# The state-space scan of a hybrid encoder step, computed feature-major: two heads in the two column halves of TensorE, the carried part in the same accumulation

## The reference, cut to what matters

```python
    w = jnp.einsum('bcign,bcjgn->bcijg', cm, bm)[..., None] * decay
    y = jnp.einsum('bcijgh,bcjghp->bcighp', w, xdt)
    ...
    y = y + jnp.einsum('bcign,bcghpn->bcighp', cm, h_in) * jnp.exp(acs)[..., None]
    ...
    y = y + d_skip.astype(jnp.float32).reshape(N_GROUPS, HEADS_PER_GROUP, 1) * xs.astype(jnp.float32)
    y = y.reshape(bsz, T, D_SSD).astype(x.dtype) * jax.nn.silu(z_b)
    y = rmsnorm(y.reshape(bsz, T, N_GROUPS, D_SSD // N_GROUPS), ...)
    o_b = y @ w_o_ssd
```

## Time and profile before

| what | value |
|---|---|
| time, median of 3 runs | 2502.21 us (2500.35 to 2502.59) |
| span of the profiled execution | 2502.9 us |
| TensorE busy, whole span | 2346.0 us (94%) |
| VectorE, ScalarE, GpSimd busy | 755.6 us (30%), 795.0 us (32%), 619.2 us (25%) |
| mean granted clock of TensorE | 0.970 |
| scan stage, first and last matmul | 1828.39 us, about 2272 us |

### The profile page before, as it was taken

The page is one execution under the profiler, slowest core; times in us unless marked ns, Lnnn a source line. Parts: engine busy times, 40 slices in busy tenths (PEclk is TensorE's granted clock), DMA queues, the critical chain, the costliest instruction groups (busy, mean ns, idle before and its releaser), DMA issues. The chain is left out here.

```text
span 2502.9 us, 35437 instructions
## 1 busy us (share of the span) xinstructions
PE 2346.0 (94%) x12807; PEld 2107.6 (84%) x12807; DVE 755.6 (30%) x1470; ACT 795.0 (32%) x1892; POOL 619.2 (25%) x547
## 2 busy tenths in 40 slices
PE   6999999999999999999999399999749999996999
PEld 5999999999999999999999278888537788774887
DVE  4211000024444000100000465555255665653221
ACT  5211111134444111221111365555245455432000
POOL 3110101110111011011010255555246655651000
PEclk9999999999999999999999599999969999998999
DMA  4311111111111212111129654444265656534432
GB/s 160 87 57 69 63 75 69 68 69 69 68 69 69 85 51 78 69 69 69 69 85 43 150 129 117 109 108 105 77 187 149 160 159 176 162 84 152 142 126 97
DMA packets 280002, 250.10 MB, mean 100 GB/s; under 512 B 74184, under 2 KB 257336, under 8 KB 272760
## 3 DMA queue, kind: packets, MB, share of 16 engines
q1 hardware_dynamic: 279944, 249.34, 35.0%
HBM read 158.35 MB, written 90.95 MB: 100 GB/s over the span
## 5 line engine op out<-in xcount | busy, mean ns | idle before, releaser
L74 PE MATMUL acc<-h_hi,w_hi 128*128 128x424 f32 (+1 forms) x2280 | 810.6, 356 | 10.1 <-DVE h_lo L547 10.1
L75 PE MATMUL acc<-h_lo,w_hi 128*128 128x424 f32 (+1 forms) x2280 | 807.5, 354 | 0.0
L76 PE MATMUL acc<-h_hi,w_lo 128*128 128x424 f32 (+1 forms) x2280 | 807.2, 354 | 0.0
L74 PEld LDWEIGHTS acc<-h_hi,w_hi 128*128 128x128 f32 x2280 | 430.3, 189 | 24.8 <-DVE h_lo L547 11.4
L75 PEld LDWEIGHTS acc<-h_lo,w_hi 128*128 128x128 f32 x2280 | 430.6, 189 | 7.3
L76 PEld LDWEIGHTS acc<-h_hi,w_lo 128*128 128x128 f32 x2280 | 430.4, 189 | 7.4
L318 POOL TENSOR_TENSOR w_lo<-w_raw,w_hi 128x1024 fp32r<-128x1024 f32 x57 | 144.7, 2539 | 1130.5 <-ACT w_hi L360 1130.5
L385 ACT ACTIVATE row<-acc 128x424 f32<-128x424 f32 (+1 forms) x215 | 112.7, 524 | 825.2 <-PE acc L76 825.1
L583 DVE SCALAR_TENSOR_TENSOR conv_acc<-conv_in,conv_wb,conv_acc 128x424 f32<-128x424 f32 (+2 forms) x216 | 126.1, 584 | 380.9 <-ACT conv_acc L430 373.1
L1113 ACT ACTIVATE a_prob<-a_score,a_neg_max 128x129 f32<-128x129 f32 x264 | 103.3, 399 | 50.3 <-DVE a_neg_max L1254 47.6
L74 PE MATMUL a_o_ps<-a_w_hi,a_at_hi 128*128 128x512 f32 (+1 forms) x272 | 117.0, 430 | 2.0 <-DVE a_branch L1287 2.0
(11 more groups left out here) (215 smaller groups left out, 3047.5 us busy)
## 6 DMA issues: line engine op xcount, KB each, us to landing
proj<-row SPq DMA_DIRECT2D x56, 1056.0 KB, 4.0
w_raw<-in_w_in_dram SPq DMA_DIRECT2D x28, 1024.0 KB, 5.1
s_feat<-proj SPq DMA_DIRECT2D x16, 1280.0 KB, 7.9
s_acs_b<-acs_dram SPq DMA_DIRECT2D x16, 1024.0 KB, 7.3
a_q_diag<-proj SPq DMA_DIRECT2D x66, 128.0 KB, 4.4
a_z<-proj SPq DMA_DIRECT2D x16, 512.0 KB, 4.8
a_gate_t<-proj SPq DMA_DIRECT2D x16, 512.0 KB, 4.6
branch_rows<-a_branch SPq DMA_DIRECT2D x16, 512.0 KB, 3.2
```

The source lines that it names most:

```text
L74: pe.matmul(out, hi, whi, start=first, stop=False)
L75: pe.matmul(out, hi, wlo, start=False, stop=False)
L76: return pe.matmul(out, lo, whi, start=False, stop=last)
```

## The change

The scan result is made with features on the partitions from the start. Each head's product has the head's 64 features as the stationary operand's columns, and even and odd heads write to partitions 0 to 63 and 64 to 127 of `y_ps`, which now has one bank for each group. The carried part goes into the same accumulation: ScalarE makes `exp(acs)` for all 16 heads on all partitions (`carried_exps`), VectorE multiplies it by C (`carried`), and each head's state times that goes into `y_ps` ahead of the chunk's part. The scaling and adding on VectorE (L1929, L1936) and the transposes (`turned`) go; `skipped` reads `y_ps`. VectorE adds the squares of four feature blocks (`square_sums`), and `squares` is one product for each group in place of four. In stage 1 one exponential and a fifth of a table go.

```diff
@@ project_inputs @@
-                    act.activation(into, acs, ACT.Exp).then_inc(exps_ready, 1)
@@ scan_states: tiles @@
-        tmp = sb("tmp", [P, BANK])
-        work = sb("work", [P, 4, D])
-        tok, yx, yg = work[:, 0, :], work[:, 1, :], work[:, 2, :]
-        y_sq = work[:, 3, :]
+        carry_c = sb("carry_c", [P, NH, P])
+        y_sum = sb("y_sum", [P, G, P])
+        work = sb("work", [P, 3, D])
+        yx, yg, y_sq = (work[:, i, :] for i in range(3))
-        y_ps = pb("y_ps", [P, BANK])
-        i_ps = pb("i_ps", [P, BANK])
+        y_ps = pb("y_ps", [P, G, BANK])
@@ SyncE: load_acs @@
                 after(sp, S["segs"], m)
-                sp.dma_start(acs_b[0:t.n, :, 0:t.n],
-                             io.acs_dram[:, bass.ds(t.col, t.n)].partition_broadcast(t.n)).then_inc(S["acs_in"], 16)
+                after(sp, S["c_exps"], m)
+                sp.dma_start(acs_b[:, :, 0:t.n],
+                             io.acs_dram[:, bass.ds(t.col, t.n)].partition_broadcast(P)).then_inc(S["acs_in"], 16)
@@ ScalarE @@
+            def carried_exps(m):
+                t = TokenTile(m)
+                act.wait_ge(S["acs_in"], 16 * m + 16)
+                after(act, S["inter_ready"], 2 * m)
+                act.activation(carry_c[:, :, 0:t.n], acs_b[:, :, 0:t.n], ACT.Exp).then_inc(S["c_exps"], 1)
...
             act.wait_ge(S["tables_in"], 16)
             decays(0, 0)
+            carried_exps(0)
...
                     decays(m + 1, 1 - slot)
                     rows_of_gb(m + 1, 1 - slot)
+                    carried_exps(m + 1)
@@ VectorE @@
-            def combine(m, slot, g):
...
+            def carried(m, slot):
+                t = TokenTile(m)
+                dve.wait_ge(S["c_exps"], m + 1)
+                dve.wait_ge(feat_in[slot], arrived(m, slot))
+                for g in range(G):
+                    v = carry_c[:, g * GH:(g + 1) * GH, 0:t.n]
+                    dve.tensor_tensor(v, v, feat[:, slot, C0 + g, 0:t.n].unsqueeze(1).to_broadcast([P, GH, t.n]),
+                                      ALU.mult).then_inc(S["c_ready"], 1)
+            def update(m, g):
                 st = state[:, stream(m), g * GF:(g + 1) * GF]
                 dve.wait_ge(S["added_ready"], 2 * m + g + 1)
                 dve.wait_ge(S["decayed"], 2 * m + g + 1)
                 dve.tensor_tensor(st, st, st_ps[:, :], ALU.add).then_inc(S["state_ready"], 1)
+            def square_sums(m):
+                t = TokenTile(m)
+                dve.wait_ge(S["ysq_ready"], 2 * m + 2)
+                after(dve, S["ss_ready"], m)
+                dve.tensor_reduce(y_sum[:, :, 0:t.n],
+                                  y_sq.rearrange("p (g k n) -> p g n k", g=G, k=GT)[:, :, 0:t.n, :],
+                                  AX.X, ALU.add).then_inc(S["ysum_ready"], 1)
             def skipped(m, slot, g):
-                dve.wait_ge(S["t_ready"], 2 * m + g + 1)
+                dve.wait_ge(S["intra_ready"], 2 * m + g + 1)
...
             masked(0, 0)
+            carried(0, 0)
             for q in range(1, 6):
                 scale_w(q)
             def step(m, slot):
-                combine(m, slot, 0)
+                if has_prev(m):
+                    square_sums(m - 1)
+                update(m, 0)
                 if has_prev(m, 2):
                     merge(m - 2, slot, 1)
-                combine(m, slot, 1)
+                update(m, 1)
                 skipped(m, slot, 0)
...
                 skipped(m, slot, 1)
                 if has_next(m):
                     times_dt(m + 1, 1 - slot, 1)
+                    carried(m + 1, 1 - slot)
                 if has_prev(m):
                     merge(m - 1, 1 - slot, 0)
@@ TensorE @@
             def core(m, slot, g):
                 after(pe, S["state_ready"], 2 * m - 2 + g + 1)
-                after(pe, S["tmp_ready"], 2 * m + g)
-                pe.matmul(i_ps[r, :], feat[:, slot, C0 + g, 0:t.n], state[:, stream(m), g * GF:(g + 1) * GF],
-                          start=True, stop=True).then_inc(S["inter_ready"], 1)
+                pe.wait_ge(S["c_ready"], 2 * m + g + 1)
+                after(pe, S["yx_ready"], 2 * m - 2 + g + 1)
+                for h in range(GH):
+                    o = slice(h % 2 * HEAD, h % 2 * HEAD + HEAD)
+                    f = g * GF + h * HEAD
+                    mm = pe.matmul(y_ps[o, g, h // 2 * P:h // 2 * P + t.n], state[:, stream(m), f:f + HEAD],
+                                   carry_c[:, g * GH + h, 0:t.n], start=(h < 2), stop=False)
+                mm.then_inc(S["inter_ready"], 1)
...
-                after(pe, S["tok_ready"], 2 * m + g)
                 for h in range(GH):
+                    o = slice(h % 2 * HEAD, h % 2 * HEAD + HEAD)
                     f = g * GF + h * HEAD
-                    mm = pe.matmul(y_ps[r, h * HEAD:(h + 1) * HEAD], mix[r, slot, g * GH + h, 0:t.n],
-                                   xdt[r, slot, f:f + HEAD], start=True, stop=True)
+                    mm = pe.matmul(y_ps[o, g, h // 2 * P:h // 2 * P + t.n], xdt[r, slot, f:f + HEAD],
+                                   mix[r, slot, g * GH + h, 0:t.n], start=False, stop=(h >= GH - 2))
...
             def gates(m, slot, h):
-                if h == 0:
-                    pe.wait_ge(g_in[slot], arrived(m, slot))
-                    after(pe, S["gate_ready"], 2 * m)
-                    pe.wait_ge(S["yx_ready"], 2 * m + 2)
-                elif t.sample:
-                    pe.wait_ge(S["gate_ready"], 2 * m + 1)
-                else:
-                    pe.wait_ge(S["yx_ready"], 2 * m + 4)
+                pe.wait_ge(g_in[slot], arrived(m, slot))
+                after(pe, S["gate_ready"], 2 * m + h)
-            def turned(m, g):
...
             def squares(m):
-                pe.wait_ge(S["ysq_ready"], 2 * m + 2)
+                pe.wait_ge(S["ysum_ready"], m + 1)
                 pe.wait_ge(S["state_ready"], 2 * min(m + 2, TILES + 1) if isinstance(m, int) else 2 * m + 4)
                 for g in range(G):
-                    for k in range(GT):
-                        f = (g * GT + k) * P
-                        mm = pe.matmul(st_ps[0:t.n, g:g + 1], y_sq[:, f:f + t.n], ones[:, 0:1],
-                                       start=(k == 0), stop=(k == GT - 1))
+                    mm = pe.matmul(st_ps[0:t.n, g:g + 1], y_sum[:, g, 0:t.n], ones[:, :], start=True, stop=True)
...
                 core(m, slot, 1)
                 if has_next(m):
                     products(m + 1, 1 - slot)
-                turned(m, 0)
                 if has_next(m):
                     x_rows(m + 1, 1 - slot, 0)
                 if has_prev(m):
                     squares(m - 1)
                 prev(run, 0, 1)
-                turned(m, 1)
```

More of the change, by code:

```diff
@@ L126, in project_inputs @@
         dt_a, t1, t2, t3 = (table(xs_flat, i) for i in range(4))
-        dt, acs, into = (table(x_more[:, :], i) for i in range(3))
+        dt, acs = (table(x_more[:, :], i) for i in range(2))
         to_end, total = (table(acc_flat, i) for i in range(2))
@@ L276, in _ @@
                     store_row(T_GA + s + 2 * q, 1 - s)
-            sp.wait_ge(exps_ready, 3)
-            sp.dma_start(io.dt_tables[:, 0:3 * NTH], x_more[:, 0:3 * NTH]).then_inc(tables_out, 16)
-            sp.dma_start(io.dt_tables[:, 3 * NTH:5 * NTH], acc_flat[:, 0:2 * NTH]).then_inc(tables_out, 16)
+            sp.wait_ge(exps_ready, 2)
+            sp.dma_start(io.dt_tables[:, 0:2 * NTH], x_more[:, 0:2 * NTH]).then_inc(tables_out, 16)
+            sp.dma_start(io.dt_tables[:, 2 * NTH:4 * NTH], acc_flat[:, 0:2 * NTH]).then_inc(tables_out, 16)
             sp.wait_ge(acs_copied, UNITS)
@@ L624, in _ @@
             dve.wait_ge(acs_ready, 1)
-            dve.wait_ge(exps_ready, 2)
+            dve.wait_ge(exps_ready, 1)
             dve.tensor_tensor(t2, xt[:, 1, 0:NTH].rearrange("p (m h) -> p m h", h=NH), acs, ALU.subtract)\
@@ L717, in acs_turn @@
             def acs_turn(b):
-                pe.wait_ge(exps_ready, 3)
+                pe.wait_ge(exps_ready, 2)
                 after(pe, acs_copied, b - 1)
@@ L1530, in scan_states @@
         state = sb("state", [P, 2, D])
-        tmp = sb("tmp", [P, BANK])
-        work = sb("work", [P, 4, D])
-        tok, yx, yg = work[:, 0, :], work[:, 1, :], work[:, 2, :]
-        y_sq = work[:, 3, :]
+        carry_c = sb("carry_c", [P, NH, P])
+        y_sum = sb("y_sum", [P, G, P])
+        work = sb("work", [P, 3, D])
+        yx, yg, y_sq = (work[:, i, :] for i in range(3))
+        final = work[:, 0:2, :].rearrange("p a (h n) -> p (a h) n", h=2)
         y_hi = sb("y_hi", [P, 2, KT, P], F32R)
@@ L1540, in scan_states @@
         raw = [w_raw[:, 0], w_raw[:, 1]] + [rows[:, i, :].rearrange("p (k n) -> p k n", k=KT) for i in range(2)]
-        tables = sb("tables", [P, 5, NTT, NH])
-        dt, acs, into, to_end, total = (tables[:, i, :, :] for i in range(5))
+        tables = sb("tables", [P, 4, NTT, NH])
```

(34 more changed lines are left out.)

13 lines of the change are left out of this document (removed).

## The result

The change made the kernel slower: 2532.51 us (median of 4, 2531.15 to 2533.79) against 2501.68 us before on the same chip; the ratio is 1.0123, 95% interval 1.0111 to 1.0136. That is 10 us above the 2522 forecast, inside the forecast's own range of 2508 to 2535. The profiled executions have spans of 2530.0 and 2502.9 us, 27.1 apart. A span is shorter than the time of the same execution: 2530.0 goes with 2531.74, and in every execution with both on record the span is 1.7 to 1.9 us shorter.

What follows compares the result with a forecast made beforehand. The prediction took TensorE to set the scan's pace before, and the wait for both behind carried after. Tiles +12.2, start +5, end -4, clock +6.5 make +20 on 2502.9; less 0.7, 2522 us; range 2494 to 2545, the forecast's own 2508 to 2535.

Steps and rivals of the forecast that it cites:

- The core: TensorE's core in each tile: column halves overlap, so it takes 2.91 us in place of 3.50.
- The pair of products: VectorE's two carried products ahead of merge: 3.72 us, including a GpSimd turn between them; bounds 2.26 and 4.5.
- The two idle stretches: TensorE in each tile: idle 2.2 us before run(m-1, 1, 0) and 2.6 us waiting for both before the last run.
- The two small edges: VectorE in each tile: no more 0.39 us wait for squares, but small product L1903 waits about as long; they cancel.
- The steady tile: One scan tile: 24.70 us, 0.94 longer; +12.2 us over 13 tiles, between -7 and +22.
- The clock: TensorE's granted clock falls after idle stretches: 0.5 us a tile, between 0 and 1.7; +6.5 in all (0 to +22).
- Rival (d): Clock falls in each tile, or both products wait in full: +1.7 us each a tile, 2535 to 2545; chance 0.12.
- Start of the stage: First steps of the scan: carried delays GpSimd's weight halves and the second step's chain is longer; +5 us (0 to 7).
- Tile 15 and the end: Tile 15, preparing the half-size sample tile, taken as 0; stage end, where TensorE leads, -4 us (-5 to -2).
- The stage behind: The stage after the scan: the prediction's sum has no term for it.
- the 0.7 that the prediction took off: End of the sum: 0.7 us subtracted for the difference between the profiled execution and the median.

Runs made afterwards that it cites:

- e3_same_half_in_a_row: The kernel after, with the heads of a group ordered 0, 2, 4, 6, 1, 3, 5, 7 so neighbours use the same column half; 2556.97 us.
- e4_gpsimd_waits_for_carried: The kernel after, with one wait more: GpSimd starts gated(m, 1) only when both carried products are done; 2506.55 us.
- e1: The kernel after, with carried(m+1) queued behind merge(m-1, 0) on VectorE instead of in front of it; 2505.74 us.
- e10: The kernel after, with rstd(m-1) in front of to_ends(m+1, 0) on GpSimd and carried left ahead of merge; 2557.97 us.
- e6_rstd_earlier: The kernel of e1 with rstd(m-1) put in front of to_ends(m+1, 0) on GpSimd; 2472.53 us.
- e5_sixteen_squares: The kernel of e1 with the squares added on TensorE as before (16 records) and square_sums left away; 2475.86 us.
- e2: The kernel after, with the carried product of group 1 left out, so VectorE has one 128x1024 product of the two; 2500.84 us.
- e8: The kernel before with only square_sums on VectorE and squares as one product a group; 2504.31 us.

## Why the prediction was right

- **The core.** Forecast 2.91, measured 2.86. The halves overlap; `e3_same_half_in_a_row` shows that the order of the heads matters.
- **The pair of products.** Forecast 3.72, measured 3.75 from start to `both` (2023.29 to 2027.04). The mechanism, GpSimd's turn between them, is shown by `e4_gpsimd_waits_for_carried`.
- **The two idle stretches.** Forecast 2.2 and 2.6, measured 2.15 and 2.42. Which one counts is shown by `e1` and `e10`. From the end of the core to the last `run` it is 12.88 us (2015.04 to 2027.92), forecast 12.84. The two small edges cancel as forecast: the wait of 0.39 us at 2009.00 is gone (so VectorE was not quite without a rest there, as the prediction has it), and the small product takes 1.07 us where it took 0.47.
- **The steady tile.** Forecast 24.70 without a fall, measured 24.87, against 23.8 on average before: 1.07 in place of 0.94, 13.9 us over 13 tiles in place of 12.2.
- **The clock.** This term was under-sized: 6.5 forecast, 9.4 measured, six tiles at 1.56 more. The 0.5 us a tile stood for a chance; in fact the falls come once a tile and cost 1.56 us in six of the 13, 0.72 a tile. That the cost is nothing behind the first idle stretch and some 1.6 behind the second was forecast; that the falls would come out about evenly between the two was not, and is luck. Rival (d) had a fall in each tile, at 1.7 us: there is one in each, and had all of them cost time, the sum would have been 11 us higher. The rule of the Trainium skill (TensorE: Matmul & The Clock Gate, What's actually happening), that the half clock follows a stretch in which TensorE was idle throughout, would have had none, and 2516; the profile shows a fall in every tile, behind idle stretches of 2.15 and 2.42 us that matmuls surround.
- **Start of the stage.** Forecast +5. From the scan's first matmul to `core(2, 0)` it is 77.35 us (1827.63 to 1904.98), where it was 71.79 (1828.39 to 1900.18): +5.6. The stages in front took 0.8 less, which is within their spread: that first matmul lies between 1822.44 and 1830.04 in the twelve profiles.
- **Tile 15 and the end.** Tile 15 was taken as 0 and gave 1.8 back (21.50 against 23.26): the pair of `carried` for the half-size sample tile takes 1.27 us there, not 3.83. The end was forecast at -4 and gave -2.0 (51.32 us from `core(16, 0)` to the next stage's first matmul, against 53.29). One cause shows in the profile: `square_sums` of the last tile stands behind a `merge`, and the product of the squares waits for it. TensorE's row, and VectorE's in the steady part, which names the reduction's length:

```profile
2279.82 0.39 PE L2104 MATMUL s_st_ps<-s_ones,s_y_sum 128*64 128x1 f32 x4 [2.08 <-DVE s_y_sum L1950]
```

```profile
2003.64 2.01 DVE L1950 TENSOR_REDUCE s_y_sum<-s_work 128x256 f32<-128x1024 f32 x1
```

- **The stage behind.** Taken as nothing; it took 2.9 us more (2310.39 to 2530.0, against 2286.22 to 2502.9). TensorE's rows give two parts. Its second block of products starts 20.36 us into the stage, where it was 19.00, behind a wait of 2.89 us, where it was 1.89; the chain leads back to ScalarE, which waits 2.19 us for the load of the weights, where it waited 1.07. Then the clock falls once more, from 2332.0 on (0.53 over 3.4 us), which it did not do before: the other 1.6 us. Why that load came later is open, and no edit here reaches this stage.

```profile
2305.22 0.50 PE L74 MATMUL o_o_ps<-o_w_hi,o_m_hi 128*128 128x512 f32 x1 [1.89 <-DVE o_w_lo L772]
```

```profile
2330.75 0.50 PE L74 MATMUL o_o_ps<-o_w_hi,o_m_hi 128*128 128x512 f32 x1 [2.89 <-DVE o_w_lo L770]
```

The first row is of the kernel before, the second of the kernel after.

The sum: -0.8 + 5.6 + 13.9 + 9.4 - 1.8 - 2.0 + 2.9 = 27.2, against 27.1 measured between the profiled executions. The medians differ by 30.8. The profiled execution of the kernel after, at 2531.74 us, lies 0.8 below its median. The one before has a span of 2502.9; if it too is 1.7 us shorter than its time, that was 2504.6, 2.9 above its median, and not the 0.7 that the prediction took off (it compared a span with times). Together these are the other 3.7 us, which would then be spread between executions and no effect of the change. The forecast was 10 us low through the clock (2.9), the stage behind (2.9), the end (2.0), the tile (1.7) and this spread, less what tile 15 and the stages in front gave back. The mechanism of the steady tile was right in each part; that the total came this close owes something to terms that cancel.

## What to carry to other kernels

Where an engine is 98% busy, count what it saves, but then follow the next two chains at the same place, in the order of their queues: here 3.3 us less work a tile became two waits, 4.6 us together, and `carried` put behind `merge` in VectorE's queue, together with one swap on GpSimd, turned 2532 into 2473 (`e6_rstd_earlier`). A product of two SBUF tensors on VectorE should not stand in front of something urgent while GpSimd's queue is full. And idle time on TensorE is not free even where another engine sets the pace: here it cost clock that the saved work did not repay (`e1_carried_behind_merge` against `e5_sixteen_squares`).

## What the hardware showed that I had not expected

- A kernel with more work on TensorE was faster: with 1.3 us more a tile in an idle stretch, and VectorE's `square_sums` gone, it took 30 us less (`e5_sixteen_squares`), some 19 of them since the clock stayed up.
- With a fall in each tile, e1, e2 and e4 all take 23.8 us a tile, though without one they take 22.2 (e1) and 22.6 (e2). The falls come 23.9 us apart there, and the tile seems to fit itself to them; why is open. It may be chance: e4 has no tile without a fall to compare, and e8 takes 23.8 with no fall at all, idle stretches of 1.74 us and all.
- A reduction over 4 values 128 apart took 2.01 us for 1024 values, where a product of 1024 values takes 1.21. The Trainium skill (Vector Engine (DVE) Microarchitecture Reference, Measured stream behaviour on trn2) gives 1.73 ns a column for a source that hops 4 KiB at each element, an estimated 1.8 us; here the hop is 512 bytes, and the row is somewhat above that.
